# A hybrid attention layer on eight cores: memory attention moved beside the first two head pairs, convolution beside the last two, and 128 transposes moved from TensorE to DMAs

## What is computed

```python
h = rmsnorm(x, g_mix)
u, c_gate, b_gate, q, k, v, q_m = split(h @ w_in)         # 512,512,512,1024,1024,1024,512 columns
y_conv = rmsnorm(b_gate * causal_conv3(c_gate * u), g_conv)
y_diff = diff_attention(rope(norm(q)), rope(norm(k)), v)  # 8 heads, two softmax maps of 64 each, v of 128
km, vm = split(rmsnorm(mem, g_mem) @ w_mem_kv)            # 256 memory rows
y_mem  = rmsnorm(cross_attention(norm(q_m), norm(km), vm), g_mem_out)   # 4 heads of 128
x = x + concat(y_conv, y_diff, y_mem) @ w_o
x = x + (silu(rmsnorm(x) @ w_gate) * (rmsnorm(x) @ w_up)) @ w_down
```

## The kernel before

| phase | attention | fill |
|---|---|---|
| 0 | pair 0 | conv 0, projection of pair 1, conv 1 |
| 1 | pair 1 | projection of pair 2, conv 2 |
| 2 | pair 2 | conv 3, projection of pair 3 with the convolution's normalisation and the memory rows woven in, memory k and v |
| 3 | pair 3 and 16 steps of memory attention (`MemAtt.step`) | the 16 q tiles of the memory part (`qm_tile`) |

## Time and profile before

### The profile page before, as it was taken

How to read it: one execution, slowest core, us unless ns; L and a number is a source line. 1 busy time by engine, 2 the same in 40 slices (tenths; PEclk the granted TensorE clock), 3 DMA queues, 4 the chain that set the end, 5 groups by cost and what they waited for, 6 DMA issues and landing times.

```text
span 3088.3 us, 44821 instructions; the slowest of 8 cores (3081.3 to 3088.3 us)
## 1 busy us (share of the span) xinstructions
PE 2954.4 (96%) x17012; PEld 1463.0 (47%) x17012; DVE 897.9 (29%) x1569; ACT 624.6 (20%) x1007; POOL 258.4 (8%) x466
## 2 busy tenths in 40 slices
PE   4999999998888899999999999999999999999999
PEld 3656555455544444444444444444444444444444
DVE  4644454446356333200023100022100022000022
ACT  3434444344566211100000000000000000000000
POOL 3412122012100000000000000000000000000000
PEclk9999999999999899999999999999999999999999
DMA  6520211221540876522279312289321299222097
GB/s 186 126 50 6 52 34 27 47 52 61 94 90 18 189 206 194 120 41 41 41 183 264 97 36 41 41 211 275 67 38 31 41 240 257 55 41 42 1 264 209
DMA packets 150482, 317.65 MB, mean 103 GB/s; under 512 B 45952, under 2 KB 60288, under 8 KB 137600
## 3 DMA queue, kind: packets, MB, share of 16 engines
q0 software_dynamic: 19584, 102.77, 19.5%
q1 hardware_dynamic: 93824, 144.90, 14.7%
q10 hardware_dynamic: 36864, 67.13, 8.1%
HBM read 317.89 MB, written 91.23 MB: 132 GB/s over the span
## 4 chain that ended last, share of the span: by engine, by line
PE 91%; DVE 4%; ACT 2%; issue 2%; DMA 2%; POOL 0%; DVEq 0%; SPq 0%; ACTq 0%; POOLq 0%
PE ps L1259 39%; PE ps L518 24%; PE ps L1294 20%; PE ps L755 3%; PE ps L738 2%; DMA arena<-x 1%; ACT arena L829 1%; DVE arena L795 1%; DMA arena<-wmix 1%; PE ps L532 1%; PE ps L496 1%; DVE arena L796 0%; DVE arena L800 0%; DVE arena L542 0%; PE ps L771 0%
## 5 line engine op out<-in xcount | busy, mean ns | idle before, releaser
L1259 PE MATMUL ps<-arena 128*128 128x512 bf16 x5632 | 1216.2, 379 | 0.0
L518 PE MATMUL ps<-arena 128*128 128x512 bf16 (+1 forms) x4224 | 855.4, 354 | 19.8 <-DVE arena L542 8.0
L1259 PEld LDWEIGHTS ps<-arena 128*128 128x128 bf16 x5632 | 551.1, 98 | 664.5
L1294 PE MATMUL ps<-arena 128*128 128x512 bf16 x2816 | 608.4, 379 | 0.0
L518 PEld LDWEIGHTS ps<-arena 128*128 128x128 bf16 x4224 | 393.8, 98 | 387.1 <-issue 80.6
L1294 PEld LDWEIGHTS ps<-arena 128*128 128x128 bf16 x2816 | 275.5, 98 | 332.2
L1266 DVE TENSOR_TENSOR arena<-ps,arena 128x1024 bf16<-128x1024 f32 x88 | 107.7, 1224 | 1109.6 <-ACT arena L1265 1109.6
L1265 ACT ACTIVATE arena<-ps 128x1024 bf16<-128x1024 f32 x88 | 90.1, 1024 | 1567.3 <-PE ps L1259 1567.3
L829 ACT ACTIVATE arena<-ps 128x1024 bf16<-128x1024 f32 (+1 forms) x304 | 292.6, 974 | 128.4 <-PE ps L738 122.7
L1297 DVE TENSOR_TENSOR arena<-ps,arena 128x512 f32<-128x512 f32 x256 | 176.6, 691 | 424.2 <-PE ps L1294 274.7
L755 PE MATMUL ps<-arena 128*128 128x129 bf16 x2176 | 175.0, 223 | 28.2 <-ACT arena L829 15.9
(11 more groups left out here) (103 smaller groups left out, 995.3 us busy)
## 6 DMA issues: line engine op xcount, KB each, us to landing
arena<-run ACTq DMA_DIRECT2D x256, 256.0 KB, 16.6
run<-arena SPq DMA_DIRECT2D x192, 256.0 KB, 11.1
arena<-wgu POOLq DMA_DIRECT2D x88, 512.0 KB, 7.2
arena<-x SPq DMA_DIRECT2D x32, 1024.0 KB, 6.0
arena<-wmix POOLq DMA_DIRECT2D x32, 1024.0 KB, 16.5
arena<-wd POOLq DMA_DIRECT2D x16, 1408.0 KB, 17.6
run<-arena SPq DMA_DIRECT2D x16, 1024.0 KB, 3.9
out<-arena SPq DMA_DIRECT2D x64, 256.0 KB, 9.7
```

What stands on the lines that cost most here:

```text
L518: ins = e.matmul(out, lhsT=l_, rhs=r_, start=(kc == 0), stop=(kc == nk - 1))
L1259: ins = e.matmul(bank(bo_ + hf), lhsT=w[:, kc, :], rhs=hT[:, kc, tsl], start=(kc == 0), stop=(kc == KC - 1))
L1294: ins = e.matmul(bank(bk), lhsT=actT[:, ci, rsl], rhs=wdv[:, ci, :], start=(ci == 0), stop=(ci == UC - 1))
```

## The change

It regroups the fill, sets new rates, and replaces all 512 TensorE transposes of the mixing part and of setup that are not `trans_rows` by DMA transposes from SP.

| phase | attention after | fill after |
|---|---|---|
| 0 | pair 0 | memory k, tiles 0 to 5 of pair 1, memory v, tiles 6 to 15, the first 4 memory q tiles |
| 1 | pair 1 and the 16 steps of memory attention | projection of pair 2 with the other 12 memory q tiles between its tiles |
| 2 | pair 2 | conv 0, projection of pair 3 |
| 3 | pair 3 | conv 1, conv 2, conv 3 |

```diff
-RATE = (2.45, 1.9, 2.2, 0.75)
+RATE = (1.62, 1.6, 1.82, 1.73)
...
+        qbs += [AR.alloc(512) for _ in range(3)]
+        bqb += [Buf("qb%d" % i) for i in range(2, 5)]
...
-        def qk_tail(dst, bdst, si, bk, off):
...
-            pe(tr, [bqb[si], bsm], [PB[bk]])
-            dve(lambda e: e.tensor_copy(dst, pv.rearrange("p (j t) -> p j t", j=4)), [PB[bk]], [bdst])
+        def qk_tail(dst, bdst, si):
+            P.op("sp", lambda e: e.dma_start(out=dst, in_=qbs[si], transpose=True), reads=[bqb[si]], writes=[bdst], dma_key="tq%d" % si)
...
             def finish(h, gp, par):
-                if not fbanks[0]:
-                    after(1, lambda: finish(h, gp, par))
-                    return
...
-                pe(tr, [bysb[par], bsm], [PB[bk]])
...
+                dst, bd = (mix3[:, h - 6, tsl], bmix3[h - 6][gp]) if h >= 6 else (mst[par], bmst[par])
+                P.op("sp", lambda e: e.dma_start(out=dst.rearrange("p (n t) -> p n t", n=4), in_=ysb[par], transpose=True), reads=[bysb[par]], writes=[bd], dma_key="ty%d" % par)
+                if h < 6:
                     P.op("sp", lambda e: e.dma_start(out=mix_d[mo][:, tsl], in_=mst[par]), reads=[bmst[par]], writes=[bmixd[mo][gp]], dma_key="mst%d" % par)
```

In the memory part the transpose of a group becomes two DMA transposes and a store, and a q tile counts as ready five ticks after its transpose is recorded:

```diff
+            def f(qi):
+                qk_tail(QmT[g % 2][:, :, n * 128:(n + 1) * 128], bQmT[g % 2][n], qi)
+                after(5, lambda: MA.got.append(t))
...
+                    for n in range(2):
+                        P.op("sp", lambda e, n=n: e.dma_start(out=yT[:, :, n * 128:(n + 1) * 128], in_=yb[:, n * 512:(n + 1) * 512], transpose=True), reads=[byb], writes=[by], dma_key="tm%d" % k)
+                    P.op("sp", lambda e: e.dma_start(out=mix_d[12:16, :, g * 256:(g + 1) * 256].rearrange("h p t -> p h t"), in_=yT), reads=[by], writes=[bmixd[12][g]], dma_key="mm%d" % k)
```

The memory rows are loaded, normalised and transposed (still on TensorE, 32 transposes) at the end of setup instead of in phase 2. The convolution keeps parts 0 to 2 in `raw_d`; part 3 goes straight into `mixT`, and each group of 512 tokens is loaded into `mixT` and scaled there, behind conv 3:

```diff
+                        P.settle("pool", bhT[4 * tg:4 * tg + 4])
+                        pool(lambda e: e.tensor_copy(mixT[:, 3, tsl], y1), [by1], [bMT[tg][1]])
+                        mix_load(tg)
...
+                    after(2, lambda: rsqrt_act(ssq[:, tg, :], ssq[:, tg, :], 512.0, [bssq[tg]], [bssq[tg]]))
+                    if tg < 3:
+                        after(8, lambda: conv_scale(tg))
```

The order around it:

```diff
+        phase(attn(0), chain_(mem_k(), lambda: (wl(22, 3), wl(23, 4)), proj(1, 0, 2, 0, 6), mem_v(), lambda: (wl(18, 3), wl(19, 4)), proj(1, 0, 2, 6),
+                              lambda: [wl(12 + i, i) for i in range(3)], qm_init, qm_first()), RATE[0])
+        phase(attn(1, MA), qm_rest(), RATE[1])
         run_due(True)
+        to_conv()
+        phase(attn(2), chain_(conv(0, 3, 4), lambda: wl(1, 3), proj(3, 0, 2), lambda: (wl(2, 0), wl(5, 1), wl(3, 2))), RATE[2])
+        wo_early()
+        phase(attn(3), chain_(conv(1, 3, 4), lambda: (wl(29, 3, 8), wl(26, 4, 8)), conv(2, 0, 1), lambda: wl(30, 0, 8),
+                              conv(3, 2, 1), lambda: (wl(27, 1, 8), wl(31, 2, 8)), conv_flush()), RATE[3])
...
+        for cg in range(3):
+            wo_mm(0, cg)
+        run_due(True)
```

More of the change, by code:

```diff
@@ L399, in build @@
         xb = [AR.alloc(D) for _ in range(2)]
+        assert AR.off <= conv_end - 4096
+        AR.off = att_base
         lamtmp = AR.alloc(64, F32)
@@ L524, in build, with head_norm @@
         pend_tr = []
-        def qk_tail(dst, bdst, si, bk, off):
[L527 to L533, removed]
-            pe(tr, [bqb[si], bsm], [PB[bk]])
-            dve(lambda e: e.tensor_copy(dst, pv.rearrange("p (j t) -> p j t", j=4)), [PB[bk]], [bdst])
-        def head_norm(bk, si, gain, ng, nd, rope_t):
-            sq, tmp, qb, st8 = sqs[si], tmps[si], qbs[si], st8s[si]
+        tcnt = [0]
+        def qk_tail(dst, bdst, si):
+            P.op("sp", lambda e: e.dma_start(out=dst, in_=qbs[si], transpose=True), reads=[bqb[si]], writes=[bdst], dma_key="tq%d" % si)
+        def head_norm(bk, si, gain, ng, nd, rope_t, tail):
+            sq, tmp, st8 = sqs[si], tmps[si], st8s[si]
+            qi = qcnt[0] % 5
+            qcnt[0] += 1
+            qb = qbs[qi]
             act(lambda e: e.activation(out=sq, in_=bank(bk), func=AF.Square), [PB[bk]], [bsq[si]])
@@ L588, in proj_tile @@
             mg = mm_group(bank(bk), lambda kc: hT[:, kc, tsl], lambda kc: wq[:, :, kc, :], 16, [bU[uqk], bU[uqk + 1], bhT[t]], bk, T512, 4)
-            for _ in range(3):
-                yield next(mg)
-            yield from mid_tr()
             yield from mg
-            rd = head_norm(bk, si, c_gqk, 8, 64, t)
-            pend_tr.append((lambda b_, off: qk_tail(QKT[:, :, tsl], bQs[s_][t], si, b_, off), rd))
+            head_norm(bk, si, c_gqk, 8, 64, t, lambda qi: qk_tail(QKT[:, :, tsl], bQs[s_][t], qi))
             bk = take()
@@ L601, in flush_tr, with proj @@
             while pend_tr:
[L602 to L607, removed]
+                yield GAP
+        def proj(hp, uqk, uv, t0=0, t1=NT):
+            for t in range(t0, t1):
                 yield from proj_tile(hp, t, uqk, uv)
-            yield from flush_tr()
+            if t1 == NT:
+                yield from flush_tr()
         bz2 = [Buf("z0"), Buf("z1")]
@@ L982, in build @@
         SCM = float(128.0 ** -0.5)
-        mixT = hT
-        bMT = [[Buf("mixT%d_%d" % (g, c)) for c in range(2)] for g in range(4)]
-        bMm = [Buf("mixM%d" % g) for g in range(4)]
         def qm_tile(t):
-            si = t % 2
+            si = tcnt[0] % 2
+            tcnt[0] += 1
             tsl = slice(t * 128, (t + 1) * 128)
@@ L1147, in build @@
+        rows = [arena_t[:, o:o + 4096].bitcast(F32) for o in (conv_end - 2 * 4096, conv_end - 3 * 4096, conv_end - 4096)]
         xb2 = [arena_t[:, scr_base:scr_base + 2048], arena_t[:, att_base - 512:att_base + 1536]]
```

291 lines of the change are left out of this document (109 added, 182 removed).

## The result

The ratio of after to before is 0.9776, 95% interval 0.9757 to 0.9794: faster by 2.24%. The profiled execution took 3018.41 us and another run 3023.19, against 3089.72 to 3091.24 before; 3015 was forecast. Some runs of every kernel have a whole die (cores 0 to 3, or 4 to 7) at a lower granted clock and a much longer time; they are left out throughout, and where an experiment has no ratio too few of its runs were left for one. The 128 of the title are the new DMAs; the transposes that they replace on TensorE are 512. In this document a transpose of one tile, group or half group, by either way, is a turn.

The account below looks back on a forecast made before the run. TensorE, busy for 96% of the span, was taken to bound the kernel. Transposes 28.7, stall 44.6 and setup 2.4 sum to 75.7 us off 3089.85: 3014, stated as 3015 for the median of runs; range 2990 to 3060.

Parts of the forecast that it names:

- The pattern: Old attention phases: less fill means more stall, from 0.15 us a step in phase 0 to 0.55 in phase 3.
- Transposes off TensorE: Setup and mixing: 512 transposes at 0.056 us each leave TensorE's bounding stream, 28.7 us counted in full.
- Regrouped fill: Phases and tail: fill spread more evenly over attention steps lowers stall from 116.6 to 72 us, a gain of 44.6.
- Phases: The four attention phases after the change: about 188, 225, 200 and 202 us.
- never-waiting work: Phases priced as if TensorE never waited: 172.2, 201.5, 186.4 and 187.8 us after the change; the rest counts as stall.
- Tail: After phase 3: it loses its memory groups and starts the output projection first, stall 4 us where it was 8.6.
- Setup, -2.4: Before phase 0: the wait for the last tile's transposition goes, 2.4 us; mem loads and two more tiles cost nothing.
- DMA turns: 128 small transposes on SP: 2.5 us to landing, 0.6 us of SP each, 77 us in all, hidden.
- Late turns (3057): Rival: turns land late and hold memory attention in phase 1, 42 us lost, 3057; chance 0.12.
- Stall that belongs to the step (3060): Rival: 304 steps keep their mean stall whatever the fill, only transposes and setup wait go, 3060; chance 0.12.
- The dense-phase case (2977): Rival: nearly all stall goes, as in dense parts of phase 0, 35 us left, 2977; chance 0.09.
- Slower (3130): Rival: memory scores in TensorE's stream wait for q tiles whose turns land at 20 us, 116 us, 3130; chance 0.05.

Follow-up runs that it names:

- early-fill kernel: New kernel with all four rates at 2.45, so each phase's fill is used up after about two thirds of its steps: 3060.57 and 3048.15, ratio 0.9838.
- regrouped kernel: New kernel with all 512 turns back on TensorE, each inside the matmuls of the tile after next: 3072.68 to 3073.13 (three more runs 3093.23 to 3115.14), ratio 0.9959.
- old grouping: Old kernel's schedule with 448 of the 512 turns as DMAs from SP and five buffers instead of two: 3052.55 to 3055.79, ratio 0.9891.
- first placement: New kernel with all 512 turns back on TensorE, each three ticks behind its tile's last DVE operation: 3082.31, one run.
- first turns-alone kernel: Old kernel's schedule and two row buffers, with 448 of the 512 turns as DMAs from SP: 3098.85 and 3122.58, against 3091.36 and 3114.25 of the old kernel.

## Why the prediction was right, point by point

**The total** is right: 75.7 us of gain forecast, 71.4 found. Part of that is luck. The phases were to give some 65 us and gave 66.4, but with phase 1 10 us longer than forecast and phases 2 and 3 4 and 9 us shorter. Setup came out 8.9 us worse, the tail 2.8 better.

- *The pattern*, "the less fill a step has, the more stall", left out phase 2, which had 1.9 us of fill a step and 0.41 of stall, more than phase 1 with 1.7 and 0.28. So fill was not all of it even in the old kernel. That steps without fill make stall is shown by the early-fill kernel, in three phases of four. The wait that I named for it, of the product for the exponent, went "down from 16 us to a few" in phase 3 and came back in phase 1, in all 19.1 us for 22.1. Idle TensorE time in the phases fell from 79.6 to 50.9 us all the same.
- *Transposes off TensorE, 28.7 us.* The slots stand by count (442 of them, 24.8 us, in the four phases of the regrouped kernel), though no run measured them apart from the waits. The banks were to free about 5 us in each of phases 1 to 3, some 15 in all, which I booked under the stall. Beyond the slots the runs have 9 us in the old grouping and 22.5 in the phases of the new one.
- *Regrouped fill, 44.6 us*, some 30 without those 15, is too much for it alone: with the turns on TensorE it gave 17, or about 21 with the first placement's phases. I had put nearly the whole fall of the stall to the fill, while the waits for banks and rows go only with the turns. This error and the one before it cancel.
- *Phases*: 188, 225, 200, 202 forecast; 189.8, 235.1, 195.8, 192.6 found. By the prediction's own never-waiting work that leaves stalls of 17.6, 33.6, 9.4 and 4.8, for 16, 24, 14 and 14. Why phases 2 and 3 do better than the 14 no run shows; the old phase 1's bank waits were already taken off it. Phase 1 is worse. Its bare end was right: 12 steps at 0.7 forecast, 14 at 0.54 found, so 7.6 us for 8.4 (the sum rounded that up to 10). Some of the rest fell at a step which named its price and then struck it out: "the memory steps should end about two thirds into phase 1 by the credit, so nothing waits. If they end last, 6 to 8 us." The last of them ends at 87% of the phase, and its group's turn then comes behind the loads that the kernel issues at that very place. With the loads moved away 2.9 of the 5.75 us of wait went, and 3.4 us of the phase: half of the price.
- *Tail*: 4 us of stall and 3.1 of work moved out would be 7.7 of gain; 10.5 were found.
- *Setup, -2.4*, failed. The wait for the last transposition did go, but "The mem loads and two more normalised tiles lie beside matmuls: nothing" is wrong on three of eight cores. They are loads of 1 MB in a stretch with a DMA share of 0.81, beside two weight loads of 1 MB, and the turn that needs them stands in TensorE's stream. The slowest core decides the time, so +6.5 us in place of -2.4. Moving the weight loads only moved the wait to the row tiles of x. No row of setup was read for that term.
- *DMA turns*: landing in 2.5 us is right to the digit, SP's 0.6 us each was 1.18. 128 of them make 151 us over some 920, still hidden. With the old kernel's two buffers the landing is visible, by the first turns-alone kernel; I never priced the three more, and together with the turn's place 12 to 26 us of setup hung on them.
- A slip that changes no term: DVE is 50% busy in the mixing stages by the earlier trace rows, not 47%.

**The rivals.** Late turns (3057): one of 8 memory groups landed late on the path and cost 3 to 4 us, at the border and not at the scores, so the mechanism is there at a twelfth of its price. Stall that belongs to the step (3060) is out by the phases and by the early-fill kernel. The dense-phase case (2977) comes true in phases 2 and 3 (stalls of 9.4 and 4.8, for 10.5 in the old phase 0) and not in the other two. Slower (3130) needed turns landing after 15 us on every group; that happened to the last, and to none at the scores.

The figure of the Trainium skill that was weighed ("VectorE: DVE Perf Modes", "The three transpose paths": 1309 ns for a block by DMA) would have given 5.2 us for a turn, an estimate from that page; the trace has 2.5. It would have changed little, since TensorE waits for none of these landings at the memory scores.

**Open**: why some cores have the long setup and others don't, and whether the cores' loads slow each other; why phases 2 and 3 stall less than the old phase 1; whether the two halves are worth more together than apart; and how the 22.5 us in the regrouped kernel with its turns on TensorE would fall with the best placement possible, since three placements gave 3073 to 3111.

## What to carry to other kernels

Work that shares the bounding engine's stream and its PSUM banks costs its slots and also the waits it brings: 442 transposes, 24.8 us of slots, made the phases 47 us longer here. Price both. When such work goes to a DMA, count its buffers, since each is held until the DMA has landed. Where a step waits for the landing of a small DMA, look at which big loads are issued just ahead of it: here they made 16.8 us of 2.5. A step may also end an engine's wait and leave another just behind it, so a wait's length is not yet the gain. A core that saves time at one place may give it back at the next shared one, and the time is that of the slowest core.

## What the runs showed of the hardware that was not expected

- A transposing DMA of 128x512 takes 1.18 us on SP's sequencer, over half of the 2.0 us of one four times its size, while its landing (2.5 us for 4.4) is also well over a quarter.
- The same turn landed after up to 29.3 us where others took 2.4, while the median hardly moves. Issued 3 us behind three 1 MB weight loads it landed after 16.8 us, and after 2.5 when these were issued later.
- The granted clock stayed down after the wait had ended: 0.85 over the ten us in which TensorE was busy throughout.
- Eight cores with the same program differ by 13 us in setup, in another pattern in each kernel, and the wait behind it follows the weight loads: near 134 us with the late ones, near 90 us with the early ones.
